# Stick-breaking attention in pairs of heads, with the mask as one fp32r product and another order of the projections

## What is computed

```python
def stick_breaking_attention(q, k, v):
    ...
        z = jnp.einsum('bqhd,bkhd->bhqk', qb, k).astype(jnp.float32) * scale
        mask = k_pos[None, :] < q_pos[:, None]
        log_beta = jax.nn.log_sigmoid(z)
        log_keep = jnp.where(mask, jax.nn.log_sigmoid(-z), 0.0)
        suffix = lax.cumsum(log_keep, axis=3, reverse=True) - log_keep
        a = jnp.where(mask, jnp.exp(log_beta + suffix), 0.0)
        return jnp.einsum('bhqk,bkhd->bqhd', a.astype(v.dtype), v)
```

## Time and profile before

| what | value |
|---|---|
| median of three runs | 1098.76 us |
| the profiled execution's own time | 1099.27 us |
| its span | 1097.5 us |
| busy: TensorE, VectorE, ScalarE | 1067.2, 680.7, 567.3 us |
| granted TensorE clock, mean of the span | 0.997 |
| stick-breaking blocks, first to last product | 805.8 to 856.1 us |

### The profile page before, as it was taken

The page is one execution under the profiler, slowest core; times in us unless marked ns, Lnnn a source line. Parts: engine busy times, 40 slices in busy tenths (PEclk is TensorE's granted clock), DMA queues, the critical chain, the costliest instruction groups (busy, mean ns, idle before and its releaser), DMA issues.

```text
span 1097.5 us, 17869 instructions
## 1 busy us (share of the span) xinstructions
PE 1067.2 (97%) x6692; PEld 934.0 (85%) x6692; DVE 680.7 (62%) x1048; ACT 567.3 (52%) x802; POOL 10.3 (1%) x15
## 2 busy tenths in 40 slices
PE   6999999999999999999999999999999999999996
PEld 5998877887999899897868999898988779889995
DVE  5797796766655655577675645655744766555553
ACT  5644744755644444454555544444645755544441
POOL 0000010000000000000000000000000000000000
PEclk9999999999999999999999999999999999999999
DMA  7754433565464566464334564565432335566531
GB/s 280 261 175 150 135 120 130 173 196 188 153 218 166 177 216 230 161 207 158 117 112 146 204 198 165 181 213 179 156 133 96 115 116 179 167 220 207 187 132 39
DMA packets 53658, 185.43 MB, mean 169 GB/s; under 512 B 5840, under 2 KB 9184, under 8 KB 53600
## 3 DMA queue, kind: packets, MB, share of 16 engines
q1 hardware_dynamic: 52544, 183.58, 50.6%
q10 hardware_dynamic: 1056, 1.06, 0.3%
HBM read 183.55 MB, written 1.07 MB: 168 GB/s over the span
## 4 chain that ended last, share of the span: by engine, by line
PE 82%; DVE 10%; ACT 4%; issue 2%; DMA 0%; DVEq 0%; SPq 0%; ACTq 0%
PE ps L402 25%; PE ps L404 25%; PE ps L403 25%; DVE wlo L1356 3%; PE ps L471 2%; ACT whi L947 1%; ACT arena L1008 1%; PE ps L544 1%; PE ps L520 1%; DVE arena L1425 1%; PE ps L595 1%; DVE arena L1479 1%; DVE stat L1478 0%; PE ps L843 0%; ACT arena L1018 0%
## 5 line engine op out<-in xcount | busy, mean ns | idle before, releaser
L1356 DVE TENSOR_TENSOR wlo<-raw,whi 128x1024 fp32r<-128x1024 f32 x339 | 405.9, 1221 | 189.3 <-ACT whi L947 188.1
L947 ACT ACTIVATE whi<-raw 128x1024 fp32r<-128x1024 f32 x339 | 348.6, 1053 | 193.2 <-PE ps L404 128.7
L402 PE MATMUL ps<-hT_hi,whi 128*128 128x256 f32 x1152 | 329.6, 286 | 0.1
L403 PE MATMUL ps<-hT_lo,whi 128*128 128x256 f32 x1152 | 326.6, 284 | 0.0
L404 PE MATMUL ps<-hT_hi,wlo 128*128 128x256 f32 x1152 | 326.5, 283 | 0.0
L402 PEld LDWEIGHTS ps<-hT_hi,whi 128*128 128x128 f32 x1152 | 221.5, 192 | 2.9 <-DVE hT_lo L1376 1.1
L403 PEld LDWEIGHTS ps<-hT_lo,whi 128*128 128x128 f32 x1152 | 221.6, 192 | 0.7
L404 PEld LDWEIGHTS ps<-hT_hi,wlo 128*128 128x128 f32 x1152 | 221.6, 192 | 0.0
L402 PE MATMUL ps<-whi,y_hi 128*128 128x512 f32 (+1 forms) x540 | 214.0, 396 | 0.7 <-DVE y_lo L1515 0.5
L404 PE MATMUL ps<-whi,y_lo 128*128 128x512 f32 (+1 forms) x540 | 209.9, 389 | 0.0
L403 PE MATMUL ps<-wlo,y_hi 128*128 128x512 f32 (+1 forms) x540 | 209.9, 389 | 0.0
(11 more groups left out here) (211 smaller groups left out, 749.9 us busy)
## 6 DMA issues: line engine op xcount, KB each, us to landing
raw<-stream SPq DMA_DIRECT2D x339, 512.0 KB, 4.2
x<-x_in SPq DMA_DIRECT2D x2, 512.0 KB, 3.7
arena<-scratch ACTq DMA_DIRECT2D x1, 1024.0 KB, 10.6
arena<-rb SPq DMA_DIRECT2D x1, 1024.0 KB, 6.3
bm<-decay SPq DMA_DIRECT2D x1, 1024.0 KB, 6.2
out<-x SPq DMA_DIRECT2D x4, 256.0 KB, 2.1
cst<-const SPq DMA_DIRECT2D x1, 906.0 KB, 10.5
arena<-gfin SPq DMA_DIRECT2D x1, 512.0 KB, 6.6
```

Of the source, the lines that this page charges most:

```text
L402: pe.matmul(o, a[0], b[0], start=start, stop=False)
L403: pe.matmul(o, a[0], b[1], start=False, stop=False)
L947: act.activation(whi[:, u % RING, :], raw[:, u % RAW, :], ACT.Copy).then_inc(sem("hi_done"), 1)
L1356: dve.tensor_tensor(wlo[:, u % RING, :], raw[:, u % RAW, :], whi[:, u % RING, :].bitcast(F32), ALU.subtract).then_inc(sem("lo_done"), 1)
```

## The change

The projection order becomes `sq`, `sk`, `cq`, `ckv`, `sv`, `uq0`, `uq1`, `kn`, `vn`. The attention goes by pairs of heads p = 0 to 3. The mask is the first product of a bank: one fp32r product of 2 x 128 columns, read from fp32r copies of unit matrix and mask that ScalarE makes once. The score products of both heads alternate between the upper and lower 64 rows and between two banks. VectorE and ScalarE work over 2 x 384 elements in each operation. The sums take two products a head. The scaled exponentials of each pair are kept in four buffers, `sba`, in memory that held the bias of the first attention of layer two. All values are multiplied in one block behind unit 20, alternating between the column halves. Scores stand behind units 8, 11, 14, 17, sums behind 10, 13, 16, 19. The latents are turned behind units 15 and 18.

```diff
-    for name, kind, cols, nkt in (("sq", "F", 512, KT), ("sk", "F", 512, KT), ("sv", "T", 512, KT),
-                                  ("cq", "T", 384, KT), ("ckv", "T", 288, KT), ("uq0", "T", 512, 3),
+    for name, kind, cols, nkt in (("sq", "F", 512, KT), ("sk", "F", 512, KT), ("cq", "T", 384, KT),
+                                  ("ckv", "T", 288, KT), ("sv", "T", 512, KT), ("uq0", "T", 512, 3),
                                   ("uq1", "T", 256, 3), ("kn", "T", 512, 2), ("vn", "T", 512, 2)):
...
+        sba = [c3(bm[:].rearrange("p a b -> p (a b)")[:, 768 * p:768 * p + 768], a=2) for p in range(4)]
...
+        unit_r = Y[0][:, 1, 3, 0:P]
+        mask_r = Y[0][:, 1, 3, P:S]
...
+        SB_SCORES = {8: 0, 11: 1, 14: 2, 17: 3}
+        SB_SUMS = {u + 2: p for u, p in SB_SCORES.items()}
...
-            def sb_scores(h):
-                g = slice(64 * (h % 2), 64 * (h % 2) + 64)
-                b = W0 + h % 2
...
-                pe.matmul(ps[:, b, 0:S], sk[g, h // 2, 0:P], sq[g, h // 2, :], start=True, stop=True)
-                pe.matmul(ps[:, b, S:S + P], sk[g, h // 2, P:S], sq[g, h // 2, P:S], start=False, stop=True,
-                          skip_group_check=True)
-                for c in (0, S):
-                    m = pe.matmul(ps[:, b, c:c + P], cs(C_ID), cs(C_ST), start=False, stop=True, skip_group_check=True)
+            def sb_scores(p):
+                if p >= 1:
+                    pe.wait_ge(sem("sb_a"), p)
+                else:
+                    pe.wait_ge(sem("sb_c"), 1)
+                for j in range(2):
+                    pe.matmul(c3(ps[:, W0 + j, :], a=2)[:, :, 0:P], unit_r, mask_r.unsqueeze(1).to_broadcast([P, 2, P]),
+                              start=True, stop=True)
+                for keys, queries in ((slice(0, P), slice(0, S)), (slice(P, S), slice(P, S))):
+                    at = keys.start + queries.start
+                    for j in range(2):
+                        g = slice(64 * j, 64 * j + 64)
+                        m = pe.matmul(ps[:, W0 + j, at:at + queries.stop - queries.start], sk[g, p, keys],
+                                      sq[g, p, queries], start=False, stop=True, skip_group_check=True)
                 m.then_inc(sem("sb_z"), 1)
...
-            def sb_sums(h):
...
-                n = sbn[:, h % 2, :]
...
-                pe.matmul(ps[:, b, 0:S], cs(C_NSUF), n[:, 0:S], start=False, stop=True, skip_group_check=True)
-                pe.matmul(ps[:, b, P:S], cs(C_NONE), n[:, S:S + P], start=False, stop=True, skip_group_check=True)
-                pe.matmul(ps[:, b, S:S + P], cs(C_NSUF), n[:, S:S + P], start=False, stop=True,
-                          skip_group_check=True).then_inc(sem("sb_r"), 1)
...
-            def sb_values(h):
-                g = slice(64 * (h % 2), 64 * (h % 2) + 64)
-                b = W2 + (h // 2) % 2
-                a = sbt[:, h % 2, :]
...
-                pe.matmul(ps[g, b, 0:S], sv[:, 0, 64 * h:64 * h + 64], a[:, 0:S], start=True, stop=True)
-                m = pe.matmul(ps[g, b, P:S], sv[:, 1, 64 * h:64 * h + 64], a[:, S:S + P], start=False, stop=True,
...
-                m.then_inc(sem("sb_v"), 1)
+            def sb_sums(p):
+                pe.wait_ge(sem("sb_n"), p + 1)
+                for j in range(2):
+                    n = sbn[:, j, :]
+                    pe.matmul(ps[:, W0 + j, 0:3 * P], cs(C_NSUF), n, start=False, stop=True, skip_group_check=True)
+                    m = pe.matmul(ps[:, W0 + j, P:S], cs(C_NONE), n[:, S:S + P], start=False, stop=True,
+                                  skip_group_check=True)
+                m.then_inc(sem("sb_r"), 1)
+            def sb_values():
+                pe.wait_ge(sem("sb_a"), 4)
+                pe.wait_ge(sem("la_lo"), 2)
+                pe.wait_ge(sem("evac"), evac_no["sv"] + 1)
+                for p in range(4):
+                    at = (p % 2) * S
+                    for t, queries in ((0, slice(0, S)), (1, slice(P, S))):
+                        a = t * P + queries.start
+                        for j in range(2):
+                            g = slice(64 * j, 64 * j + 64)
+                            m = pe.matmul(ps[g, W2 + p // 2, at + queries.start:at + S],
+                                          sv[:, t, 128 * p + 64 * j:128 * p + 64 * j + 64],
+                                          sba[p][:, j, a:a + queries.stop - queries.start],
+                                          start=t == 0, stop=True, skip_group_check=True)
+                    if p % 2:
+                        m.then_inc(sem("sb_v"), 1)
...
-            seq = [(n, k) for n in ("sq", "sk", "sv", "cq", "ckv", "uq0", "uq1", "kn", "vn")
+            seq = [(n, k) for n in ("sq", "sk", "cq", "ckv", "sv", "uq0", "uq1", "kn", "vn")
...
-                if u == 10:
-                    pe.wait_ge(sem("evac_v"), evac_v_no["sk"])
-                    sb_scores(0)
-                if 11 <= u < 19:
-                    h = u - 11
-                    sb_sums(h)
-                    if h == 1:
-                        pe.wait_ge(sem("evac"), evac_no["sv"] + 1)
-                    if h >= 1:
-                        sb_values(h - 1)
-                    if h < 7:
-                        sb_scores(h + 1)
-                if u == 19:
-                    sb_values(7)
-                if u in (17, 20):
-                    c = 0 if u == 17 else 1
+                if u in SB_SCORES:
+                    if u == 8:
+                        pe.wait_ge(sem("evac_v"), evac_v_no["sk"])
+                    sb_scores(SB_SCORES[u])
+                if u in SB_SUMS:
+                    sb_sums(SB_SUMS[u])
+                if u == 20:
+                    sb_values()
+                if u in (15, 18):
+                    c = 0 if u == 15 else 1
                     pe.wait_ge(sem("la_n"), c + 1)
                     if c:
...
-                        pe.wait_ge(sem("sb_lo"), 3)
+                        pe.wait_ge(sem("la_lo"), 1)
...
+            def sb_first(p):
+                act.wait_ge(sem("sb_m"), p + 1)
+                link(act.activation(sbt, sbt, ACT.Exp))
+                act.activation(sbt, sbt, ACT.Ln, bias=bias1).then_inc(sem("sb_l"), 1)
+            def sb_second(p):
+                act.wait_ge(sem("sb_r"), p + 1)
+                act.activation(sba[p], ps[:, W0:W0 + 2, 0:3 * P], ACT.Exp).then_inc(sem("sb_a"), 1)
+            def sb_hi(c):
+                act.wait_ge(sem("sb_v"), c + 1)
+                act.activation(Y[0][:, 0, 2 * c:2 * c + 2, :], c3(ps[:, W2 + c, :], a=2), ACT.Copy).then_inc(sem("sb_hi"), 1)
...
-                if 12 <= u < 20:
-                    sb_second(u - 12)
-                if 11 <= u < 19:
-                    sb_first(u - 11)
-                if u in (14, 16, 18, 20):
-                    sb_hi((u - 14) // 2)
-                if u in (18, 21):
-                    la_hi(0 if u == 18 else 1)
+                if u == 2:
+                    act.wait_ge(sem("c_in"), 16)
+                    act.activation(unit_r, cs(C_ID), ACT.Copy)
+                    act.activation(mask_r, cs(C_ST), ACT.Copy).then_inc(sem("sb_c"), 1)
+                if u - 1 in SB_SUMS:
+                    sb_second(SB_SUMS[u - 1])
                 if u in (16, 19):
-                    c = 0 if u == 16 else 1
+                    la_hi(0 if u == 16 else 1)
+                if u - 1 in SB_SCORES:
+                    sb_first(SB_SCORES[u - 1])
+                if u == 21:
+                    sb_hi(0)
+                    sb_hi(1)
+                if u in (13, 17):
+                    c = 0 if u == 13 else 1
                     rsqrt(rs20[:, 2 * c:2 * c + 2], nt20[:, 2 * c:2 * c + 2], "la_v", c + 1, "la_r")
...
-                if u in (15, 18):
-                    la_squares(0 if u == 15 else 1)
+                if u in (11, 14):
+                    la_squares(0 if u == 11 else 1)
...
+            def sb_first(p):
+                dve.wait_ge(sem("sb_z"), p + 1)
+                dve.tensor_scalar(sbt, ps[:, W0:W0 + 2, 0:3 * P], 30.0, None, ALU.min).then_inc(sem("sb_m"), 1)
+            def sb_second(p):
+                dve.wait_ge(sem("sb_l"), p + 1)
+                dve.tensor_tensor(sbn, sbt, ps[:, W0:W0 + 2, 0:3 * P], ALU.max).then_inc(sem("sb_n"), 1)
+            def sb_split(c):
+                dve.wait_ge(sem("sb_hi"), c + 1)
+                dve.tensor_tensor(Y[1][:, 0, 2 * c:2 * c + 2, :], c3(ps[:, W2 + c, :], a=2),
+                                  Y[0][:, 0, 2 * c:2 * c + 2, :].bitcast(F32), ALU.subtract).then_inc(sem("sb_lo"), 1)
...
-                if 11 <= u < 19:
-                    sb_first(u - 11)
-                    sb_second(u - 11)
-                if u in (18, 21):
-                    la_lo(0 if u == 18 else 1)
-                if u not in (16, 19):
+                if u - 1 in SB_SCORES:
+                    sb_first(SB_SCORES[u - 1])
+                if u in (16, 19):
+                    la_lo(0 if u == 16 else 1)
```

(55 more changed lines are left out.)

15 lines of the change are left out of this document (removed).

## The result

The changed kernel takes 1084.3 us (median of four runs, 1083.99 to 1084.73) against 1098.68 for the kernel before beside it (median of four): the ratio is 0.987, with a 95% interval of 0.9853 to 0.9888. The forecast was 1086.9 with a range down to 1085.0.

The account below looks back on a forecast made before the run. TensorE was taken as the bound. Blocks cost 29.3 us before and 16.7 after; less 0.7 for a grown wait, 11.9 us saved, so 1098.76 - 11.9 = 1086.9 us, range 1085.0 to 1091.4.

Parts of the forecast that it names:

- The pair chain: VectorE and ScalarE work between a pair's scores and sums: 4.1 us, hidden by two units, 0.2 to spare at pair 0.
- rival D: Units 9 to 20: ScalarE's in-order queue holds conversions beyond their six-unit lead, TensorE waits; 1099 to 1100 us, chance 0.03.
- The wait that moved to the queries' transposes: Behind the values, VectorE's conversions, splits and query rotation delay TensorE; 0.6 to 0.7 us more than before, 0.7 taken.
- Rival C: Row halves overlap fully too and the wait before the queries' transposes stays as before: 1085.6 us, chance 0.15.
- what the blocks cost before: Heads' fp32 blocks between units: 25.5 us for eight heads, 2.8 waits, 0.9 returns to fp32r, 0.1 for two blocks; 29.3.
- scores and mask, four pairs, with the return to fp32r: Per pair, mask 0.24, score products 0.64 and 0.41, return 0.09: 1.38; four pairs 5.5 us where 10.6 were.
- values, with start and return: One block of sixteen products, column halves overlapping fully: 3.0 us plus 0.1 for the return, where 6.3 were.
- transposes as a block of their own: Latents' transposes behind units 15 and 18; the first becomes a block of its own, costing 0.1 us.
- Sums, per pair: Two products a head in place of three, same columns: 2.0 us a pair, 8.0 in all where 8.6 were.
- V + 7.4: Start of the queries' transposes, V being the end of the values, against V + 6.8 before the change.
- rival A: Scores and values: array halves overlap less than the nearest rows say; without any overlap 5.8 us given back, 1092.7, chance 0.08.

Follow-up runs that it names:

- the extra products: Three extra fp32 products over the whole array added to the changed kernel, between the value pairs or all ahead of their block: 1087.05 and 1085.57 us.

## Why the prediction was right in kind and short in size

**What was right.** TensorE is the bound and the stream's length is the time: the window up to the values shows no idle time left, and the mask alone, undone in the changed kernel, gave back 2.85 us where 2.4 were forecast. (Done in the kernel before it gave 2.3, of which a good third is shorter waits.) The pair chain took 3.9 us for pair 0, where 4.1 were reckoned, and is hidden by two units and not by one (6.4 us when undone, against 6.1 forecast). No ring ran dry: rival D had no part. The wait that moved to the queries' transposes came where it was placed, with 0.54 us idle. Rival C was the closest: the row halves overlap fully, and the time lies 1.3 us below the 1085.6 of C, above all as the sums were 1.0 us cheaper, which C doesn't have. The Trainium skill (TensorEngine Tiling (Array Packing), Theoretical Speedup) gives up to 2x for dimensions up to 64; the trace agrees for the streaming itself, 0.65 us for the 384 columns of two heads.

**Which terms were mis-sized.** The changed stretch saved 14.2 us by the traces, 2.3 more than the sum. Term by term:

| term of the sum | forecast | by the traces |
|---|---|---|
| what the blocks cost before | 29.3 | 29.5 |
| scores and mask, four pairs, with the return to fp32r | 5.5 | 4 x (1.18 + 0.11) = 5.2 |
| sums, four pairs, with the return | 8.0 | 4 x (1.66 + 0.09) = 7.0 |
| values, with start and return | 3.1 | 2.85 + 0.10 = 2.95 |
| transposes as a block of their own | 0.1 | 0.1 |
| wait behind the values, against before | 0.7 | (852.48 - 842.27) - (867.96 - 858.01) = 0.26 |
| saved | 11.9 | 14.0 |

The 29.5 are the ten blocks one by one in the timeline of the kernel before, from the end of a unit's last product to the next unit's first, 28.7, and 0.08 for each return; the 0.2 left over against 14.2 are not assigned to a term. (858.01 and 867.96 are the starts of unit 21 and of the keys' transposes in the timeline of the kernel before.)

The step that failed is "**Sums, per pair**": "0.09 + 0.68 + 0.22 + 0.68 + 0.22 = 1.89, plus 0.03 for the end and the return of 0.09". It took L851 from the block of the earlier trace rows, and that block begins behind a wait. What it calls the start of the block is a price of the wait, and the same step forecast that the wait would go. The run with sums one unit behind brings wait and 0.1 back together. The streaming was taken a little too long as well: four cycles of 2.4 GHz a column make 0.43 us for 256 columns and 0.64 for 384, not 0.45 and 0.68; the records have 0.43 and 0.65. And the end and the return were counted twice: the last record of 128 columns is followed 0.03 us later by the next unit's first product, which is then 0.09 longer than usual; together they are what the record would have taken anyway. That is 0.26 a pair, 1.0 us of the 2.3.

The next in size is the wait behind the values, 0.26 us where 0.7 were taken (see below). Then comes the score pair. The 0.64 of the earlier trace rows is 0.43 of streaming at full overlap and about 0.2 for entering and leaving the halved array; set against the 0.96 of two products of 96 rows it looked like an overlap of 1.5x only. Both terms of the sum, 0.64 for the products of 256 columns and 0.41 for those of 128, hold that 0.2, so their 1.05 counts it twice. In one block the products take 0.85: 0.65 of streaming, and the 0.2 only once. The mask takes 0.33 and not 0.24, since the step into the halved array stands behind it.

**What the sum did not count by itself** is that change. It has a return to fp32r and a start, and the rest is hidden in its rows. By form: a column of plain fp32 costs 0.218 / 128 us (two records of 0.109). Before, 8 heads x 1536 columns make 20.9 us; after, 4 pairs x 1792 columns and 4 x 0.24 of mask make 13.2. So 7.7 of the 14.2 us are columns: 2.5 the mask, 2.6 the scores side by side, 2.6 the values. The waits before the sums give 2.8. The moved wait takes 0.3 back, so 4.0 remain. By the prices measured, most of them are changes of array form; this part is an estimate from counts and prices, as no run undoes the changes of the kernel before alone. A head before had three inside its block (whole to column halves for the values, to row halves for the scores, to whole for the mask), 26 in all with the first and last blocks; after there are 10. At 0.17 by the extra products, or 0.2 by the single records of the scores, 16 fewer are 2.7 to 3.2 us; the seven starts behind waits give another 0.7. Between 0.1 and 0.6 us stays unassigned. The prediction carried these prices inside its rows without counting them, so most of its terms came out nearly right for reasons that were incomplete. The Trainium skill (TensorEngine Tiling (Array Packing), Key Properties) says that changing the tiling mode drains TensorE. The runs agree that a change costs time, 0.17 us each.

**The wait at the end** came where it was placed and a little smaller: the transposes begin at V + 7.06 (849.33 - 842.27) and not V + 7.4, since VectorE's conversion ended at V + 2.92 and not V + 3.0, the splits took 1.2 and not 1.3, the rotation 2.8 and not 2.9, and the handover 0.15 and not 0.2. That is 0.34. The other 0.1 is that V + 7.4 against V + 6.8 is 0.6, and 0.7 was taken. The "0.2 of waiting" that the prediction read before the queries' transposes in the kernel before isn't there; what was there is the 0.33 before unit 22, with a start dearer by 0.1, and 0.70 from the end of a product to the transposes stand in their place.

**The range** was too narrow at its lower end. It took in a full overlap but not an error of the sum's own method: the start of the sums and the overlap of the scores, both read from rows with a wait or a change of form in them, erred to the same side. Two slips of hundredths don't matter beside that: 4 x 0.67 + 0.15 is 2.83 and not 2.85, and the 5.8 of rival A is 5.7.

## What to carry to other kernels

Price a product from a row that has the same neighbours as it will have, and look at what stands ahead of it: behind a wait or behind another array form a product of TensorE is 0.1 to 0.2 us dearer than in the stream. Where short products of different forms alternate, count the changes of form beside the columns; here 16 changes fewer are an estimated 2.7 to 3.2 us, beside 7.7 for the columns. For two halves of the array to work side by side their products had to stand within two fp32 products of each other (measured for column halves; for row halves two were tried, and not more), with no product over the whole array between them; the order inside that reach was free. And look where the chain on the other engines starts: with products in row halves last, ahead of the next unit, the chain gained 0.17 us on that unit.

## What the runs showed of the hardware

Three things had not been expected. Products in two row halves or two column halves ran side by side even when the program has them one head after the other; the reach in column halves was two fp32 products (842.356 against 842.350 above). A change between whole array and column halves cost 0.17 us each, measured with products that were otherwise the same; in row halves it was 0.19 (1.5 us for eight changes). And side by side each half streams at full pace: in the values' block one pair follows the other by 0.65 us in the single records (840.219 to 840.869), which is what the 384 columns of one head take alone, 0.43 + 0.22.
